# Second stack of a six-layer model: gate columns in one block, f32r row spreads, GpSimd sums for the mLSTM denominator

## What is computed

```python
# SSD, per head: dt of 8 heads, a running sum of dt * a, and decayed scores
dt = softplus(dt_raw + dt_bias); a_cs = cumsum(dt * a)
lmat = exp(where(causal, a_cs[l] - a_cs[s], -inf))
y = einsum(cb, lmat, xdt)
# mLSTM, per head (4 of them): input gate i, forget gate f, a running sum and a running maximum
g = gate_raw + gate_b; i = g[:, :4]; f = log_sigmoid(g[:, 4:])
b = cumsum(f); m_row = max(...)            # stabiliser
w = exp(b[l] - b[s] + i[s] - m_row[l])
s = (q @ k.T) * w
h = (s @ v) / max(abs(sum(s)), exp(-m_row))
```

## Time and profile before

| | us |
|---|---|
| median of 3 runs | 2455.49 (2453.6 to 2457.11) |
| the profiled execution | 2456.62 |
| its span, first to last instruction | 2454.8 |

### The profile page before, as it was taken

The page is one execution under the profiler, slowest core; times in us unless marked ns, Lnnn a source line. Parts: engine busy times, 40 slices in busy tenths (PEclk is TensorE's granted clock), DMA queues, the critical chain, the costliest instruction groups (busy, mean ns, idle before and its releaser), DMA issues.

```text
span 2454.8 us, 30388 instructions
## 1 busy us (share of the span) xinstructions
PE 2271.3 (93%) x11815; PEld 1734.1 (71%) x11815; DVE 1571.7 (64%) x2615; ACT 862.2 (35%) x1818; POOL 456.6 (19%) x625
## 2 busy tenths in 40 slices
PE   2989999999998999999899898999989989999997
PEld 2767777778776677777768675676767776657676
DVE  7576775873586767658746576745754647766482
ACT  2433252533224643343424433214231534232331
POOL 1313121420015532011200104002220000310040
PEclk7999999999998999999999999999999999999998
DMA  7450556043571005411212121221221211122121
GB/s 235 138 159 4 137 138 152 5 137 112 120 173 34 1 10 146 129 52 37 84 52 86 36 70 34 69 69 52 86 75 63 86 53 52 35 69 70 56 82 52
DMA packets 222546, 199.50 MB, mean 81 GB/s; under 512 B 85859, under 2 KB 205507, under 8 KB 222147
## 3 DMA queue, kind: packets, MB, share of 16 engines
q1 hardware_dynamic: 210883, 155.60, 22.1%
q0 software_dynamic: 11520, 41.95, 5.6%
HBM read 194.39 MB, written 2.10 MB: 80 GB/s over the span
## 4 chain that ended last, share of the span: by engine, by line
PE 71%; DVE 15%; ACT 6%; POOL 4%; issue 2%; DMA 1%; SPq 0%; DVEq 0%; ACTq 0%; POOLq 0%
PE bank L536 17%; PE bank L537 17%; PE bank L538 17%; PE bank L675 5%; PE bank L716 3%; PE bank L689 2%; POOL h_parts L2485 2%; DVE wring_parts L1630 2%; DVE qb L2212 1%; DVE whi_parts L1629 1%; PE bank L841 1%; PE bank L973 1%; DVE bank L1758 1%; ACT pr L1305 1%; DVE mix L1933 1%
## 5 line engine op out<-in xcount | busy, mean ns | idle before, releaser
L537 PE MATMUL bank<-h_parts,whi_parts 128*128 128x512 f32 (+2 forms) x1248 | 498.6, 400 | 0.0
L1630 DVE TENSOR_TENSOR wring_parts<-wring,whi_parts 128x2048 fp32r<-128x2048 f32 (+1 forms) x126 | 285.6, 2267 | 4.3
L537 PEld LDWEIGHTS bank<-h_parts,whi_parts 128*128 128x128 f32 (+2 forms) x1248 | 233.0, 187 | 60.2 <-issue 1.2
L1629 DVE CAST whi_parts<-wring 128x2048 fp32r<-128x2048 f32 (+1 forms) x126 | 152.8, 1212 | 154.3 <-PE bank L538 130.4
L537 PE MATMUL bank<-mix_parts,whi_parts 128*128 128x512 f32 x512 | 202.4, 395 | 0.0
L536 PE MATMUL bank<-vt_parts,whi_parts 128*128 128x512 f32 (+2 forms) x456 | 187.6, 412 | 5.9 <-DVE wring_parts L1630 5.9
L538 PE MATMUL bank<-vt_parts,wring_parts 128*128 128x512 f32 (+2 forms) x456 | 182.0, 399 | 0.0
L1758 DVE CUSTOM_DVE_ANT_0 bank<-bank,causal 128x256 f32<-128x256 f32 (+3 forms) x256 | 120.5, 512 | 68.0 <-PE bank L675 66.4
L536 PE MATMUL bank<-pt_parts,whi_parts 128*128 128x512 f32 x368 | 152.0, 413 | 11.0 <-ACT kb L1214 5.3
L538 PE MATMUL bank<-mix_parts,wring_parts 128*128 128x512 f32 (+1 forms) x392 | 155.1, 396 | 0.0
L536 PE MATMUL bank<-mix_parts,whi_parts 128*128 128x512 f32 (+1 forms) x392 | 155.0, 395 | 0.0
(11 more groups left out here) (415 smaller groups left out, 5015.3 us busy)
## 6 DMA issues: line engine op xcount, KB each, us to landing
wring<-in_w_in SPq DMA_DIRECT2D x60, 1024.0 KB, 5.2
mix<-in_ada_w POOLq DMA_DIRECT2D x80, 512.0 KB, 4.7
wring<-in_w_out SPq DMA_DIRECT2D x16, 1024.0 KB, 4.8
wring<-in_mla_w_in SPq DMA_DIRECT2D x10, 1024.0 KB, 5.3
wring<-in_mla_w_out SPq DMA_DIRECT2D x8, 1024.0 KB, 4.8
wring<-in_swa_w_in SPq DMA_DIRECT2D x32, 256.0 KB, 4.4
wring<-in_nsa_w_in SPq DMA_DIRECT2D x32, 256.0 KB, 4.3
wring<-in_nsa_w_in SPq DMA_DIRECT2D x6, 1024.0 KB, 5.5
```

The costliest lines, as they stand in the source:

```text
L537: pe.matmul(bank, lh, rl, start=False, stop=False)
L1629: chain(dve.tensor_copy(high, whole))
L1630: dve.tensor_tensor(low, whole, high.bitcast(F32), ALU.subtract).then_inc(done, 1)
```

## The change

1. **One block for all row gates.** Unit `ssd_dt` becomes `row_gates`: three pieces of 32 columns, starting at dt, at the input gates and at the forget gates. PE makes one block of 96 columns where it made the block of 8; `ml_g`, its load, its two blocks and one `prepare()` are gone. ScalarE copies three pieces of the bank: the two mLSTM ones to partitions 64 to 67 of `ex`, dt to partitions 0 to 7. The biases are loaded to partitions 32 and 64 of `hcol`. All mLSTM row work is on partitions 64 to 67.
2. **Spreads in one f32r pass.** VectorE splits 32 partitions of the log rows into a high part (same partitions) and a low part (the next 32), three times a layer: inside the SSD convolutions at block 2, inside the mLSTM convolutions at blocks 2 and 4. `row_spread` multiplies these 64 partitions with a repeated column of a new small matrix `row_of`, which is built once from the identity. It serves "seg", "mseg" and "em".
3. **mLSTM weights summed by GpSimd.** GpSimd adds the parts of `pt` that the second to fourth ones-matmul read into `den_sum`, three additions of 384, 256 and 128 columns (`ml_sum`), and PE does one ones-matmul of 128 and one of 384 columns, after a wait for `den_summed`. GpSimd's order becomes: masks of head 0, then for each head the masks of the next head and the sums of this one.

```diff
-    [("ssd_dt", [(0, S0 + 1024, 8)])]
+    [("row_gates", [(0, S0 + 1024, 32), (32, M0 + 2048, 32), (64, M0 + 2048 + ML_H, 32)])]
...
-    [("ml_g", [(0, M0 + 2048, 8)])]
-    + [(("ml_qk", i), [(0, M0 + 256 * i, 256)]) for i in range(4)]
+    [(("ml_qk", i), [(0, M0 + 256 * i, 256)]) for i in range(4)]
...
-                block_of(A, (L, "dt"), weights(L, "ssd_dt"), 0, hk, m=SSD_H)
-                used(A.filled((L, "dt")))
+                block_of(A, (L, "rows"), weights(L, "row_gates"), 0, hk, m=ROWS_AT[-1] + 32)
+                used(A.filled((L, "rows")))
...
-                def log_rows(key, e, n, at):
+                def row_spread(bank, e, at, rows):
+                    return pe.matmul(bank[:, :], row_of[rows, e:e + 1].to_broadcast([64, P]), ex_parts[rows, at, :], start=True, stop=True)
+
+                def log_rows(key, e):
 
                     bank = open_bank(V, (L, key, e))
-                    pe.matmul(bank[:, :], ident[0:n, e:e + 1].to_broadcast([n, P]), rowbuf[0:n, at, :], start=True, stop=True).then_inc(V.full, 1)
...
+                    row_spread(bank, e, 0, slice(0, 64) if key == "seg" else slice(64, P)).then_inc(V.full, 1)
...
-                slots = weights(L, "ml_g")
-                for w in range(2):
-                    bank = open_bank(A, (L, "mg", w))
-                    for k in range(KC):
-                        mm = product(bank[0:ML_H, :], [t[:, k, 4 * w:4 * w + 4] for t in by_chunk(slots)], hk(k), k == 0, k == KC - 1)
-                    mm.then_inc(A.full, 1)
-                used(A.filled((L, "mg", 1)))
...
+                    row_spread(bank, e, 2, slice(64, P)).then_inc(A.full, 1)
                     pe.wait_ge(*V.emptied((L, "ms", e, NT - 1)))
                     cnt(w_ready, NT)
                     bank = open_bank(O, (L, "mo_", e))
                     causal_values(bank, e, lambda j: vt[:, j, e * P:(e + 1) * P], False, True).then_inc(O.full, 1)
+                    pe.wait_ge(*cnt(den_summed))
                     bank = open_bank(V, (L, "qn", e))
-                    causal_values(bank, e, lambda j: ones[:, :], False, True).then_inc(V.full, 1)
+                    pe.matmul(bank[:, 0:P], ones[:, :], pt[:, e % 2, 0, 0:P], start=True, stop=True)
+                    pe.matmul(bank[:, P:], ones[:, :], den_sum, start=True, stop=True).then_inc(V.full, 1)
...
+                def split_rows(first, of, to):
+
+                    high, low = slice(first, first + 32), slice(first + 32, first + 64)
+                    dve.tensor_copy(ex_parts[high, to, :], rowbuf[high, of, :]).then_inc(row_high, 1)
+                    dve.wait_ge(*cnt(row_high))
+                    dve.tensor_tensor(ex_parts[low, to, :], rowbuf[high, of, :], ex_parts[high, to, :].bitcast(F32), ALU.subtract).then_inc(rows_split, 1)
+                    dve.wait_ge(*cnt(rows_split))
...
+                def ml_sum(e):
+
+                    pool.wait_ge(*V.emptied((L, "ms", e, NT - 1)))
+                    if e:
+                        pool.wait_ge(*V.filled((L, "qn", e - 1)))
+                    pool.tensor_tensor(den_sum, pt[:, e % 2, 0, P:], pt[:, e % 2, 1, P:], ALU.add).then_inc(pool_step, 1)
+                    pool.wait_ge(*cnt(pool_step))
+                    pool.tensor_tensor(den_sum[:, P:], den_sum[:, P:], pt[:, e % 2, 2, 2 * P:], ALU.add).then_inc(pool_step, 1)
+                    pool.wait_ge(*cnt(pool_step))
+                    pool.tensor_tensor(den_sum[:, 2 * P:], den_sum[:, 2 * P:], pt[:, e % 2, 3, 3 * P:], ALU.add).then_inc(den_summed, 1)
```

More of the change, by code:

```diff
@@ L1159, in _ @@
                 ml_gate(1)
-                log_rows("mseg", 2, ML_H, 2)
+                log_rows("mseg", 2)
                 ml_scores(1)
@@ L1538, in _ @@
                 act.wait_ge(*cnt(mixed, 4))
-                for w in range(2):
-                    act.wait_ge(*A.filled((L, "mg", w)))
-                    act.activation(rowbuf[0:ML_H, 2 * w, :], A.take((L, "mg", w))[0:ML_H, :], ACT.Identity,
-                                   bias=hcol[0:ML_H, l, 2 + w:3 + w]).then_inc(A.empty, 1)
-                log1p_exp(ML_H, 3)
+                log1p_exp(ml_rows, 3)
                 for b in range(8):
@@ L1908, in late_constants @@
             def late_constants():
+                for r in (0, 64):
+                    chain(dve.tensor_tensor(row_of[r:r + 64, :], ident[r:r + 64, r:r + 8], ident[r:r + 64, r + 32:r + 40], ALU.add))
                 dve.wait_ge(*cnt(act_step, 2))
```

93 lines of the change are left out of this document (57 added, 36 removed).

## The result

Twenty runs of the changed kernel have a median of 2441.90 us (2429.41 to 2459.31), twenty of the kernel before 2458.76 (2453.5 to 2484.16): ratio 0.9921, 95% interval 0.9898 to 0.9944. The kernel is faster by 0.8%, but the forecast of 2419.0 is too low by 22.9, and its range ended at 2433. The profiled executions took 2432.01 and 2456.62, a gain of 24.6 where I had forecast 36.5.

What follows compares the result with a forecast made beforehand. PE, busy 93% of the span, was taken as the bound. Per layer 3.85 (SSD) + 9.4 (gates) + 5.5 (mLSTM heads) - 0.5 (clock) = 18.25, 36.5 for two: 2455.49 - 36.5 = 2419.0 us, range 2409 to 2433.

Steps and rivals of the forecast that it cites:

- Head loop, 4.9 a layer: SSD head loop: seven one-pass spreads save 1.9 and 3.0 us, the eighth nothing; together 4.9 a layer.
- rival two: Log-row spreads: the new spread is not one pass, giving 2433.3 us; chance 0.08.
- rival one: Whole kernel: all work that leaves PE, 57.0 us, leaves the time, giving 2398.5; chance 0.07.
- Clock behind the SSD wait: After the 3.1 us SSD convolution wait: clock read as 0.79 over 8.0 us, a loss of 1.7.
- SSD wait, 1.05: Last SSD convolution: VectorE's row split, copy plus subtraction, lengthens PE's wait by 1.05 us a layer.
- mLSTM convolution, 9.4: mLSTM convolution: dropping the old gate block's 11.5 us gains 9.4 a layer after VectorE's late units.
- mLSTM heads, 5.5: mLSTM heads: cheaper denominators and spreads gain 5.5 us a layer, partly hidden behind VectorE; no wait for GpSimd's sums.
- rival four: Ahead of the second ones-product: GpSimd's sum sits on the path, giving 2456 us and above; chance 0.02.
- Clock, 0.5: mLSTM convolution: one clock drop behind the new 2.5 us wait, mostly hidden, costs 0.5 a layer.
- Rival three: Behind convolution wait, late units, SSD wait and final chain: changed waits bring clock drops, giving 2435 us; chance 0.12.

Runs made afterwards that it cites:

- e2: Kernel before plus only row splits and f32r spreads (old gate blocks, no GpSimd sums); median 2447.43 us, ratio 0.9937.
- e3: Kernel before plus only the common gate block (f32 spreads, four ones-products, no row splits or sums); median 2437.76 us, ratio 0.9892.
- e1: Changed kernel with VectorE's weight split at head 2 of the SSD loop moved to head 4; median 2429.11 us, ratio 0.9857.
- e7: Kernel of e4 with all row splits off VectorE: ScalarE copies the high part, GpSimd subtracts; median 2427.32 us, ratio 0.9867.
- e8: Kernel of e4 with only the SSD row split moved to ScalarE and GpSimd, one block later than in e7; median 2426.44 us, ratio 0.9886.
- a4: Kernel of e4 run once more, unchanged; median 2426.08 us, ratio 0.9877.
- e4: Changed kernel with weight splits moved from head 2 to head 4 and from head 6 behind the last SSD output; median 2436.05 us, ratio 0.9868.

## Why the prediction was wrong

The sum said 36.5 over two layers; the stages gave 25.7. Term by term:

- **Head loop, 4.9 a layer: the step that failed.** The gain of the spreads was nearly right, 4.3 (e2) where I had 4.9. A single f32r spread takes 0.43 to the next instruction (1642.64 to 1643.07 in the changed kernel), 0.62 less than 1.05 where I took 0.75; the first three give 1.8 (0.96 for the three against 2.77) and four more 2.5, together the 4.3. One pass it is, so rival two is out; and with the waits that came, rival one too. What failed is the sentence that VectorE's two calls "that took the gate unit and unit one now take one and two", with only its use to PE counted and nothing for what else it does. A 64-column split at head 2 became a 2048-column one, and the quicker spreads, also my own, moved its start ahead of GpSimd's last two products of head 1; either alone costs nothing (e3, e2). It cost 3.9 a layer (47.0 against 43.1 in e1), 7.8 over two. With the 0.6 a layer by which the spreads gave less, and 1.5 back because the stretch at the lower clock in the first layer's loop didn't return at its old place, that makes 2.4 instead of 9.8 over two layers: 7.4 of the 10.8 missing.
- **Clock behind the SSD wait: 2.0 missing.** From the convolution's transpose to the first spread the stage grew by 0.8 and 1.2. The granted clock over the 10 us there:

```profile
1482.00:1492.00 10.00, 9.54 (x34) 6.71 (x34) 7.65 (x22) 0.00 (x0) 0.00 (x0) 0.72 0.00 0
```

  That is a loss of 2.8. The kernel before has 0.81 over the 9 us behind its wait, a loss of 1.7:

```profile
1479.00:1488.00 9.00, 8.92 (x33) 5.76 (x34) 7.19 (x21) 0.00 (x0) 0.00 (x0) 0.81 0.00 0
```

  I had read the wrong place. The 0.79 of the earlier trace rows is a second stretch, in the head loop, and between the two the clock was 1.00 (1488 to 1490). I priced nothing for a longer wait. The stage isn't steady: 8.46 to 9.47 in the profiles with the longer wait, so much of the 2.0 can be gone in another profile.
- **SSD wait, 1.05: right**, the stage grew by 1.16 and 1.17, since the row split is 0.42 and 0.68 with the gaps. e7 and e8 add that it can't be had back by moving it to GpSimd.
- **mLSTM convolution, 9.4: nearly right**, 8.85 and 8.82. VectorE's first convolution starts at +15.1 (1556.84 less 1541.77; forecast +14.9), unit three at +25.3 after a wait of 2.34 (forecast +25.0 and 2.5), units four and five wait 0.51 (forecast 0.6). The missing 0.55 is 0.3 by which unit three starts later, and just under 0.1 each in unit three, unit four (12.0, forecast 11.9) and the value blocks (22.6, forecast 22.5).
- **mLSTM heads, 5.5: nearly right**, 5.4 and 4.5, mean 5.0; the layer with 5.4 had the clock at 0.88 over the first 14 us and the other had 0.76, as both layers have in the kernel before (0.76 over 1620.4 to 1634.4), so 4.5 is the gain at equal clock. PE never waits for the sums, so rival four is out. What took over in part is GpSimd's low part of the mixed rows: four waits a layer in the output products, of which PE's timeline shows the first and the last here.

```profile
1693.03 0.47 PE L542 MATMUL bank<-h_parts,whi_parts 128*128 128x512 f32 x1 [0.66 <-POOL mix_parts L2544]
...
1697.47 0.50 PE L542 MATMUL bank<-h_parts,whi_parts 128*128 128x512 f32 x1 [0.73 <-POOL mix_parts L2544]
```

GpSimd's timeline beside them, 1.48 a row:

```profile
1691.50 5.91 POOL L2544 TENSOR_TENSOR mix_parts<-mix,h_parts 128x512 fp32r<-128x512 f32 x4 [5.88 <-DVE h_parts L2382]
```

- **Clock, 0.5: absent** behind the waits of the mLSTM convolution (1.00), so 1.0 comes back. The stretches that did come were in the head loops, behind the new wait, and are in the 3.9 above.

Together 7.4 + 2.0 + 0.2 + 1.1 + 1.0 - 1.0 = 10.7 of the 10.8. The median missed by 22.9. Of that 10.8 is in the two layers, 9.9 is the distance from the profile's 2432.01 to 2441.90, which comes from the upper group of runs, and 2.2 is small change: 1.1 that the profiled execution lost outside the two layers, and 1.1 by which I had started from a median below the profile. The weight of the upper group no row of one profile could have told, and my range left it out. The lower group alone lies just inside the upper end of the range (2432.01 of 2433), which would have been luck: the head loop is as wrong there. Rival three (more waits and clock drops, 2435) was nearest to the profile and partly right: 2.0 behind the SSD waits and 1.6 twice in the loops are clock, some 5, less the 1.5 that the first layer's loop got back. But in the loops the stretches stand behind a wait that it did not name, and behind the late units, which it did name, there was none.

## What to carry to other kernels

When an edit makes a VectorE copy or a two-input VectorE operation longer, or moves it, look at what GpSimd does in that window, at the times at which it will run with all parts of the edit in place, and price the overlap as a stall of whichever comes second, and of what waits behind it: here 3.9 us a layer for a split of 3.5. Moving the row split from VectorE to GpSimd gained nothing here, where VectorE was busy throughout with such operations; 1.0 of 1.1 came back. And where the times of a kernel fall in groups, compare the stages that the edit touches before the medians.

## What was not expected of the hardware

- GpSimd's product of 128 columns took 2.5 us beside a VectorE subtraction, 0.45 without; one of 256 columns 1.7 beside a copy, 0.72 without.
- The other way round, GpSimd's 1.28 us subtraction lengthened VectorE's subtraction from 2.29 to 3.37 and a group of three convolution steps from 2.33 to 3.32, though it works on 32 partitions only.
- A stretch of 30 to 50 us at 1.2 GHz in a stage in which PE never idled (PEclk 0.50 and 0.51 with PE busy for the whole window), in some executions of the same program and not in others: 14.5 us in a4 against e4. It goes with a second group of times 15 to 20 us above the first.
- A wait of 2.3 was followed by a granted clock of 0.64 over 3 us in one kernel and 1.00 in another, at the same place of the program, and the first 14 us of the mLSTM heads ran at 0.88 in one layer and 0.76 in the other of the same execution.
